# Chunked scan of the second model: first inverse built earlier, outer products spread over the levels

## The chip, the cores and the metric

The kernel runs on one core of a Trainium2 chip. The metric is the device time of one execution in microseconds (us). TensorE does the matrix products into PSUM banks, VectorE and ScalarE (ACT) work on PSUM and SBUF, SyncE issues DMAs. The engines meet through semaphores alone.

## The reference, cut to what matters

Two models of two layers each run one after the other, over 512 tokens of width 1024. The second one's layers contain a recurrence over time for eight heads of size 64:

```
state = state * w_t - (state . kk_t) (a_t * kk_t) + v_t k_t
y_t   = state . r_t
```

The kernel computes it in chunks of 64 tokens. Inside a chunk the tokens depend on each other through a strictly triangular 64 x 64 matrix A per head (products of kk and a*kk), and the chunk needs the inverse of (1 + A). With it, U = inverse x (kk . state + AK . v), the new state = (state + k v - b U) x decay, and y = r . state + PK . v - PB . U, where AK, PK and PB are masked products ("outer" ones) of k or b with kk or r. Nothing of this is left out in either kernel.

## The kernel before, in words

`scan` is called once in each of the second model's two layers, so twice in an execution. Two of the eight heads lie on the two halves of the 128 partitions ("h"), the other factor is four pairs ("pr"). Four groups g of two chunks (cc = 0, 1) are worked off; both chunks of a group are inverted together, then the state passes through them one after the other. TensorE's and VectorE's orders are written out by hand: `pe_part` and `dve_part` are the two queues, and each engine takes its instructions in that order, waiting at semaphores. ACT only copies y out (L2797).

The steps by line, all matmuls being 64 x 64 fp32:
- L2716, `products(g, bank)`: 16 matmuls into one bank: A (bank 0), its transpose (1), AK (2), PK (3), PB (4). An fp32 matmul leaves two records in the trace, so one call is 32 records, a half of it 16.
- L2808: A is masked into SBUF. L2812 and L2813 cut out the first level of A and its transpose for one chunk, L2815 makes the first inverse of it (identity minus that) into XX[cc], which holds the inverse and its transpose side by side, 256 columns each.
- L2820 to L2822: AK, PK and PB are masked into SBUF; `outer` says that TensorE has made them, `prod_used` that they have been read.
- Levels: the inverse doubles its block size five times (2 to 32). For each: L2735, W = A x inverse (8 matmuls a chunk), L2828, W is masked; L2743 and L2745, the two products that give the correction of the inverse and of its transpose (8 matmuls each, a chunk); L2831, it is subtracted, 512 columns wide. x_ok counts inverses ready, w_ok masked Ws.
- Serial part, for each chunk: L2756 and L2758 right-hand side, L2837 copy, L2768 U, L2839 copy, L2780 and L2782 state product, L2841 add, L2843 multiply with the decay (s_ok). L2703 to L2705, `y_pairs`, are the products for y, dealt out over the waits. The next group's products 0, 1 and 2 are put there too.

Between the groups the queues have, in this order: TensorE: y of chunk 1, a wait for ACT's copy of y, outer products 3 and 4 of the next group, first W. VectorE: state multiply, mask of A, both first inverses, the three outer masks, first W mask. In the diff's PSUM use, bank 5 is W of chunk 0 and right-hand side, 7 is W of chunk 1 and state product, 6 is X of chunk 0 and U, 1 is X of chunk 1 and A's transpose.

Of the kernel before, what the change touches and what calls it, by code (L numbers as in the profile page):

```python
# [10 lines left out]
ALU = mybir.AluOpType  # L11
# [4 lines left out]
P = 128  # L16
# [19 lines left out]
CH = 64  # L36
NCH = S // CH
NP = 4
# [47 lines left out]
class Core:  # L86
# [11 lines left out]
    def sem(self, name):  # L98

        if name not in self.sems:  # L100
            if name not in self.idle and self.made < self.MOST:
                self.idle[name] = self.ctx.enter_context(self.nc.semaphore(name))
                self.made += 1
            self.sems[name] = self.idle.pop(name if name in self.idle else next(iter(self.idle)))
        if name not in self.used and not name.startswith(self.LASTING):
            self.used.append(name)
        return self.sems[name]
# [2074 lines left out]
class Second(Kernel):  # L2182
# [490 lines left out]
    def scan(self):  # L2673
# [3 lines left out]
        nc, core, ps, A = self.nc, self.core, self.ps, self.arena  # L2677
# [16 lines left out]
        units = [(cc, pr, h) for cc in (0, 1) for pr in range(NP) for h in (0, 1)]  # L2694
        pairs = [(pr, h) for pr in range(NP) for h in (0, 1)]
        cols = lambda cc, pr: slice((cc * NP + pr) * CH, (cc * NP + pr) * CH + CH)

        def y_pairs(g, cc, pr):

# [6 lines left out]
            return last  # L2706

        def pe_part(pe):
            def products(g, bank):

                for cc, pr, h in units:
                    q, col = self.halves(h), (cc * NP + pr) * CH
                    tok = slice((2 * g + cc) * CH, (2 * g + cc) * CH + CH)
                    r, k, b, kk = (A[q, x + pr, tok] for x in (self.R, self.K, self.B, self.KK))
                    lhs, rhs_ = ((b, kk), (kk, b), (k, kk), (k, r), (b, r))[bank]
                    last = nc.tensor.matmul(ps[q, bank, col:col + CH], lhs, rhs_, start=True, stop=True)  # L2716
                return last
# [4 lines left out]
            products(0, 2)  # L2722
            pe.wait_ge(sem("tm_used"), 12)
            for g in range(4):
                if g:
                    pe.wait_ge(y_used, 2 * g)
                products(g, 3)
                products(g, 4).then_inc(outer, 1)

                for n, lv in enumerate(LEVELS):  # L2730
                    for cc in (0, 1):
                        pe.wait_ge(x_ok, 12 * g + 2 * n + cc + 1)
                        for pr, h in pairs:
                            q, col, o = self.halves(h), cols(cc, pr), slice(pr * CH, pr * CH + CH)
                            last = nc.tensor.matmul(ps[q, w_bank[cc], o], AT[q, col], XX[cc][q, o],  # L2735
                                                    start=True, stop=True)
                        last.then_inc(w_ps, 1)
                    for cc in (0, 1):
                        pe.wait_ge(w_ok, 10 * g + 2 * n + cc + 1)
                        for pr, h in pairs:  # L2740
                            q, col, o = self.halves(h), cols(cc, pr), slice(pr * CH, pr * CH + CH)
                            ot = slice(256 + pr * CH, 256 + pr * CH + CH)
                            nc.tensor.matmul(ps[q, x_bank[cc], o], XX[cc][q, ot], W[q, col],  # L2743
                                             start=True, stop=True)
                            last = nc.tensor.matmul(ps[q, x_bank[cc], ot], W[q, col], XX[cc][q, ot],  # L2745
                                                    start=True, stop=True)
                        last.then_inc(x_ps, 1)
# [52 lines left out]
        def dve_part(dve):  # L2800
            tt_, stt_ = nc.vector.tensor_tensor, nc.vector.scalar_tensor_tensor
            half = lambda v, cc: v.rearrange("p (c n) -> p c n", c=2)[:, cc, :]
            dve.wait_ge(sem("tm_turned"), 12)
            nc.vector.memset(state[0], 0.0).then_inc(s_ok, 1)
            for g in range(4):
                dve.wait_ge(prod, g + 1)
                dve.drain()
                tt_(as3(AT), as3(ps[:, 0, :]), wide(self.c("upper")), ALU.mult)  # L2808
                level1 = self.c("level1").unsqueeze(1).to_broadcast([P, NP, CH])
                level1t = self.c("levelT1").unsqueeze(1).to_broadcast([P, NP, CH])  # L2810
                for cc in (0, 1):
                    tt_(as3(half(XX[cc], 0)), as3(half(ps[:, 1, :], cc)), level1, ALU.mult)  # L2812
                    tt_(as3(half(XX[cc], 1)), as3(half(ps[:, 0, :], cc)), level1t, ALU.mult)  # L2813
                    dve.drain()
                    tt_(as3(XX[cc]), wide(self.c("ident2")), as3(XX[cc]), ALU.subtract)  # L2815
                    dve.drain().then_inc(x_ok, 1)
                dve.wait_ge(outer, g + 1)
                if g:
                    dve.wait_ge(y_ps, 2 * g)
                tt_(as3(AKT), as3(ps[:, 2, :]), wide(self.c("upper")), ALU.mult)  # L2820
                tt_(as3(PKT), as3(ps[:, 3, :]), wide(self.c("upper_eq")), ALU.mult)
                stt_(as3(PBT), as3(ps[:, 4, :]), -1.0, wide(self.c("upper_eq")), ALU.mult, ALU.mult)  # L2822
                dve.drain().then_inc(prod_used, 1)
                for n, lv in enumerate(LEVELS):
                    level = self.c(f"level{lv}").unsqueeze(1).to_broadcast([P, NP, CH])
                    for cc in (0, 1):
                        dve.wait_ge(w_ps, 10 * g + 2 * n + cc + 1)
                        tt_(as3(half(W, cc)), as3(ps[:, w_bank[cc], 0:256]), level, ALU.mult).then_inc(w_ok, 1)  # L2828
                    for cc in (0, 1):
                        dve.wait_ge(x_ps, 10 * g + 2 * n + cc + 1)  # L2830
                        tt_(XX[cc], XX[cc], ps[:, x_bank[cc], :], ALU.subtract)  # L2831
                        dve.drain().then_inc(x_ok, 1)
                for cc in (0, 1):
                    c = 2 * g + cc
                    old, new = state[cc], state[1 - cc]
                    dve.wait_ge(r_ps, c + 1)
                    nc.vector.tensor_copy(rhs, ps[:, 5, 0:256]).then_inc(r_ok, 1)  # L2837
                    dve.wait_ge(u_ps, c + 1)
                    nc.vector.tensor_copy(U[cc], ps[:, 6, 0:256]).then_inc(u_ok, 1)  # L2839
                    dve.wait_ge(s_ps, c + 1)  # L2840
                    tt_(new, old, ps[:, 7, 0:256], ALU.add)  # L2841
                    dve.drain()
                    tt_(as3(new), as3(new), egl[:, :, c:c + 1].to_broadcast([P, NP, CH]), ALU.mult)\  # L2843
                        .then_inc(s_ok, 1)

        return Parts(None, pe_part, act_part, dve_part)


# [603 lines left out]
```

## Time and profile before

| | |
|---|---|
| three runs, median | 3784.06 us (3781.48 to 3784.39) |
| profiled execution | 3784.52 us |
| its span in the trace | 3782.7 us |
| TensorE busy | 3664.8 us, 97% |
| VectorE busy | 2174.3 us, 57% |
| ACT busy | 1367.3 us, 36% |
| mean granted clock of TensorE | 0.982 |
| the two scans | about 2284 to 2427 us and 3139 to 3282 us |

The profile is one execution seen by the hardware profiler. A timeline row gives start, duration, engine, line, operation, operands, and in brackets how long the engine was idle before and what released it. Rows of several records (x16) give the stretch that they fill together; the last matmul's end is modelled. DMA hardly moves in the scans. The 1.8 us between the span and the execution's time lie around the program.

### The profile page before, as it was taken

The page shows a single profiled execution, that of the slowest core. Times are in us where ns is not written, and L with a number is a line of the kernel's source. Part 1 is how long each engine was busy: PE and PEld are TensorE (multiplying, and loading weights), DVE is VectorE, ACT ScalarE, POOL GpSimd, SP SyncE. Part 2 cuts the span into 40 slices and gives each one's busy share as a digit, 9 for nine tenths or more (in the row PEclk, how much of TensorE's full clock was granted, in tenths as well). Part 3 has the DMA queues.
Part 4 walks back from the last instruction along what each step waited for, and adds up shares of the span by engine and source line. Part 5 has one row for each costly group of instructions (what it writes and reads, how often), then busy time and mean ns, then how long its engine had stood idle before and what let it go on. Part 6 is the DMA issues. An engine that isn't in the chain of part 4 may idle for free. (4 is left out here: it accounts for less than half of the span.)

```text
span 3782.7 us, 57931 instructions
## 1 busy us (share of the span) xinstructions
PE 3664.8 (97%) x24033; PEld 3028.9 (80%) x24033; DVE 2174.3 (57%) x2934; ACT 1367.3 (36%) x1537; POOL 0.2 (0%) x4
## 2 busy tenths in 40 slices
PE   7999999999999999999999998999999998899998
PEld 6788888888877888888887768888887768888887
DVE  6898466774369964667634565553234575553233
ACT  5554433432264544343323341133223351123223
POOL 0000000000000000000000000000000000000000
PEclk9999999999999999999999999999999999999999
DMA  3322223553322222245522420123232320032321
GB/s 112 87 73 62 78 89 110 202 189 122 94 78 81 67 68 78 94 151 189 198 89 71 132 79 26 36 101 99 90 100 81 111 99 26 25 111 89 100 94 73
DMA packets 272985, 364.68 MB, mean 96 GB/s; under 512 B 22428, under 2 KB 218640, under 8 KB 271504
## 3 DMA queue, kind: packets, MB, share of 16 engines
q1 hardware_dynamic: 247824, 311.45, 25.7%
q10 hardware_dynamic: 24960, 50.33, 3.8%
q8 instruction: 153, 2.51, 0.3%
q14 instruction: 48, 0.39, 0.0%
HBM read 351.79 MB, written 9.96 MB: 96 GB/s over the span
## 5 line engine op out<-in xcount | busy, mean ns | idle before, releaser
L248 PE MATMUL banks<-act_hi,w_hi 128*128 128x512 f32 x4208 | 1675.2, 398 | 32.1 <-issue 9.9
L250 PE MATMUL banks<-act_hi,w_lo 128*128 128x512 f32 x4208 | 1647.9, 392 | 0.0
L249 PE MATMUL banks<-act_lo,w_hi 128*128 128x512 f32 x4208 | 1647.5, 392 | 0.0
L170 DVE TENSOR_TENSOR w_lo<-w_raw,w_hi 128x2048 fp32r<-128x2048 f32 (+1 forms) x280 | 629.4, 2248 | 666.8 <-ACT w_hi L164 662.6
L248 PEld LDWEIGHTS banks<-act_hi,w_hi 128*128 128x128 f32 x4208 | 795.5, 189 | 237.1 <-issue 59.0
L250 PEld LDWEIGHTS banks<-act_hi,w_lo 128*128 128x128 f32 x4208 | 794.7, 189 | 169.9
L249 PEld LDWEIGHTS banks<-act_lo,w_hi 128*128 128x128 f32 x4208 | 796.0, 189 | 165.1 <-issue 4.3
L164 ACT ACTIVATE w_hi<-w_raw 128x2048 fp32r<-128x2048 f32 (+1 forms) x280 | 526.5, 1881 | 932.8 <-PE banks L250 891.4
L2064 DVE SCALAR_TENSOR_TENSOR arena<-arena,small 128x512 f32<-128x512 f32 (+1 forms) x168 | 126.3, 752 | 15.6 <-issue 4.3
L248 PE MATMUL banks<-w_hi,act_hi 128*128 128x256 f32 x384 | 110.3, 287 | 3.2 <-DVE w_lo L170 3.2
L249 PE MATMUL banks<-w_lo,act_hi 128*128 128x256 f32 x384 | 108.6, 283 | 0.0
L250 PE MATMUL banks<-w_hi,act_lo 128*128 128x256 f32 x384 | 108.6, 283 | 0.0
L2797 ACT ACTIVATE arena<-banks 128x256 f32<-128x256 f32 x16 | 6.1, 383 | 279.2 <-PE banks L2705 279.2
L2743 PE MATMUL banks<-arena 64*64 64x64 f32 x1280 | 85.1, 229 | 14.9 <-DVE arena L2828 14.9
L2984 DVE TENSOR_TENSOR arena<-banks,arena 128x512 f32 (+1 forms) x44 | 30.4, 692 | 117.0 <-PE banks L250 116.3
L2743 PEld LDWEIGHTS banks<-arena 64*64 64x64 f32 x1280 | 78.2, 139 | 16.0 <-DVE arena L2828 16.0
L1869 ACT ACTIVATE arena<-banks 128x512 f32<-128x512 f32 (+3 forms) x64 | 28.1, 438 | 164.6 <-PE banks L1832 164.6
L2745 PE MATMUL banks<-arena 64*64 64x64 f32 x1280 | 83.3, 225 | 0.0
L2053 DVE SCALAR_TENSOR_TENSOR arena<-arena,param_cols 128x512 f32<-128x512 f32 x96 | 72.2, 752 | 19.0 <-issue 18.4
L2023 ACT ACTIVATE arena<-banks 128x512 f32<-128x512 f32 x48 | 28.7, 599 | 149.0 <-PE banks L250 148.7
L2050 DVE TENSOR_SCALAR arena<-arena,param_cols 128x512 f32<-128x512 f32 x48 | 26.2, 547 | 96.1 <-ACTq L2025 94.0
L695 DVE TENSOR_TENSOR act_lo<-arena,act_hi 128x1024 fp32r<-128x1024 f32 (+1 forms) x64 | 76.0, 1187 | 7.7 <-ACT act_hi L690 7.4
(363 smaller groups left out, 3592.7 us busy)
## 6 DMA issues: line engine op xcount, KB each, us to landing
w_raw<-in_w_in SPq DMA_DIRECT2D x98, 1024.0 KB, 5.4
w_raw<-in_ffn_up SPq DMA_DIRECT2D x48, 1024.0 KB, 5.4
arena<-in_ada_w ACTq DMA_DIRECT2D x24, 2048.0 KB, 8.0
w_raw<-in_w_gu SPq DMA_DIRECT2D x44, 1024.0 KB, 5.0
w_raw<-in_ffn_down SPq DMA_DIRECT2D x24, 1024.0 KB, 4.8
w_raw<-in_w_down SPq DMA_DIRECT2D x20, 1024.0 KB, 5.0
w_raw<-in_w_out SPq DMA_DIRECT2D x16, 1024.0 KB, 4.9
w_raw<-in_w_branch SPq DMA_DIRECT2D x12, 1024.0 KB, 5.0
```

Source lines behind the costliest of these rows:

```text
L164: self.core.nc.scalar.activation(view(self.hi[:, s]), view(self.raw[:, s]), ACT.Copy)\
L170: self.core.nc.vector.tensor_tensor(view(self.lo[:, s]), view(self.raw[:, s]), view(self.hi[:, s]).bitcast(FP32), ALU.subtract)\
L248: nc.tensor.matmul(out, wh, ah, start=first, stop=False)
L249: nc.tensor.matmul(out, wh, al, start=False, stop=False)
L250: return nc.tensor.matmul(out, wl, ah, start=False, stop=last)
L695: k.nc.vector.tensor_tensor(k.lo[:, self.at(i, s), :], self.source(i, s), k.hi[:, self.at(i, s), :].bitcast(FP32), ALU.subtract).then_inc( ...
L2023: nc.scalar.activation(pad[t][:, 3:3 + S], ps[:, t, :], ACT.Copy)\
L2053: ins = nc.vector.scalar_tensor_tensor(g[t], pad[t][:, 1 + k:1 + k + S], w[k], g[t], ALU.mult, ALU.add)
L2064: ins = nc.vector.scalar_tensor_tensor(dst, ada_w[:, k, :], c_act[:, k:k + 1], acc, ALU.mult, ALU.add)
L2743: nc.tensor.matmul(ps[q, x_bank[cc], o], XX[cc][q, ot], W[q, col], start=True, stop=True)
L2745: last = nc.tensor.matmul(ps[q, x_bank[cc], ot], W[q, col], XX[cc][q, ot], start=True, stop=True)
L2984: nc.vector.tensor_tensor(dst, ps[:, 2 + t, :], g[t], ALU.mult).then_inc(used, 1)
```

## The change

- The next group's mask of A and both first inverses go from the start of the group into the serial part of the group before, between its copies and adds (`a_mask`, `first_level`, `first_inverse`). Group 0 has them in front, as before.
- Outer products 3 and 4 are halved and each half is put between W of chunk 0 and W of chunk 1 in levels 0 to 3. With them goes the wait for ACT's copy of y. The first W of chunk 1 now waits for the state, because it shares bank 7.
- The three outer masks are put behind the W masks of levels 0, 2 and 4 (`outer_mask`).
- The last level leaves out L2743, the product for the inverse that isn't transposed, since only the transposed one is used afterwards; its subtraction is 256 columns wide.

The diff, cut to its core:

```diff
         def pe_part(pe):
...
             for g in range(4):
-                if g:
-                    pe.wait_ge(y_used, 2 * g)
-                products(g, 3)
-                products(g, 4).then_inc(outer, 1)
-
                 for n, lv in enumerate(LEVELS):
                     for cc in (0, 1):
+                        if cc and n < 4:
+                            if g and n % 2 == 0:
+                                pe.wait_ge(y_used, 2 * g - 1 + n // 2)
+                            last = products(g, 3 + n // 2, units[n % 2 * 8:n % 2 * 8 + 8])
+                            if n % 2:
+                                last.then_inc(outer, 1)
                         pe.wait_ge(x_ok, 12 * g + 2 * n + cc + 1)
+                        if g and cc and n == 0:
+                            pe.wait_ge(s_ok, 2 * g + 1)
...
-                            nc.tensor.matmul(ps[q, x_bank[cc], o], XX[cc][q, ot], W[q, col],
-                                             start=True, stop=True)
+                            if n < LAST:
+                                nc.tensor.matmul(ps[q, x_bank[cc], o], XX[cc][q, ot], W[q, col],
+                                                 start=True, stop=True)
...
         def dve_part(dve):
+            def a_mask(g):
+                dve.wait_ge(prod, g + 1)
+                tt_(as3(AT), as3(ps[:, 0, :]), wide(self.c("upper")), ALU.mult)
+
+            def first_level(cc):
+                tt_(as3(half(XX[cc], 0)), as3(half(ps[:, 1, :], cc)), level1, ALU.mult)
+                tt_(as3(half(XX[cc], 1)), as3(half(ps[:, 0, :], cc)), level1t, ALU.mult)
+
+            def first_inverse(cc):
+                dve.drain()
+                tt_(as3(XX[cc]), wide(self.c("ident2")), as3(XX[cc]), ALU.subtract)
+                dve.drain().then_inc(x_ok, 1)
+
+            def outer_mask(g, n):
+
+                if n == 0:
+                    tt_(as3(AKT), as3(ps[:, 2, :]), wide(self.c("upper")), ALU.mult)
+                elif n == 2:
+                    dve.wait_ge(outer, 2 * g + 1)
+                    if g:
+                        dve.wait_ge(y_ps, 2 * g)
+                    tt_(as3(PKT), as3(ps[:, 3, :]), wide(self.c("upper_eq")), ALU.mult)
+                elif n == 4:
+                    dve.wait_ge(outer, 2 * g + 2)
+                    stt_(as3(PBT), as3(ps[:, 4, :]), -1.0, wide(self.c("upper_eq")), ALU.mult, ALU.mult)\
+                        .then_inc(prod_used, 1)
...
             for g in range(4):
...
                         tt_(as3(half(W, cc)), as3(ps[:, w_bank[cc], 0:256]), level, ALU.mult).then_inc(w_ok, 1)
+                    outer_mask(g, n)
+                    new = slice(256 if n == LAST else 0, 512)
                     for cc in (0, 1):
                         dve.wait_ge(x_ps, 10 * g + 2 * n + cc + 1)
-                        tt_(XX[cc], XX[cc], ps[:, x_bank[cc], :], ALU.subtract)
+                        tt_(XX[cc][:, new], XX[cc][:, new], ps[:, x_bank[cc], new], ALU.subtract)
                         dve.drain().then_inc(x_ok, 1)
...
                     nc.vector.tensor_copy(rhs, ps[:, 5, 0:256]).then_inc(r_ok, 1)
+                    if cc and g < 3:
+                        first_inverse(0)
                     dve.wait_ge(u_ps, c + 1)
                     nc.vector.tensor_copy(U[cc], ps[:, 6, 0:256]).then_inc(u_ok, 1)
+                    if g < 3:
+                        if cc:
+                            first_level(1)
+                            first_inverse(1)
+                        else:
+                            a_mask(g + 1)
                     dve.wait_ge(s_ps, c + 1)
...
                         .then_inc(s_ok, 1)
+                    if cc == 0 and g < 3:
+                        first_level(0)
```

## Rows read from the trace of the kernel before

**Rows 1.** The page, part 1: busy time, share of the span, instructions
```profile
PE 3664.8 (97%) x24033; PEld 3028.9 (80%) x24033; DVE 2174.3 (57%) x2934; ACT 1367.3 (36%) x1537; POOL 0.2 (0%) x4
```

**Rows 2.** Timeline of VectorE, serial stage: start, us, line, [idle before <-releaser]
```profile
2314.38 0.42 DVE L2841 TENSOR_TENSOR arena<-arena,banks 128x256 f32<-128x256 f32 x1 [1.44 <-PE banks L2782]
...
2316.59 0.42 DVE L2837 COPY arena<-banks 128x256 f32<-128x256 f32 x1 [1.29 <-PE banks L2758]
...
2317.80 0.42 DVE L2839 COPY arena<-banks 128x256 f32<-128x256 f32 x1 [0.78 <-PE banks L2768]
...
2320.17 0.42 DVE L2841 TENSOR_TENSOR arena<-arena,banks 128x256 f32<-128x256 f32 x1 [1.95 <-PE banks L2782]
2320.68 0.43 DVE L2843 TENSOR_TENSOR arena<-arena,small 128x256 f32<-128x256 f32 x1
```

**Rows 3.** Timeline of VectorE, prologue of group 1
```profile
2321.19 0.69 DVE L2808 TENSOR_TENSOR arena<-banks,consts 128x512 f32<-128x512 f32 x1
2321.80 0.41 DVE L2812 TENSOR_TENSOR arena<-banks,consts 128x256 f32<-128x256 f32 x1
...
2327.14 0.76 DVE L2828 TENSOR_TENSOR arena<-banks,consts 128x256 f32<-128x256 f32 x2
```

**Rows 4.** Timeline of TensorE, the same stretch
```profile
2312.26 1.15 PE L2716 MATMUL banks<-arena 64*64 64x64 f32 x32
...
2321.26 0.28 PE L2705 MATMUL banks<-arena 64*64 64x64 f32 x2
...
2327.62 0.34 PE L2743 MATMUL banks<-arena 64*64 64x64 f32 x4 [1.91 <-DVE arena L2828]
```

**Rows 5.** Timeline of both engines, the second level of group 0
```profile
2295.14 0.68 PE L2735 MATMUL banks<-arena 64*64 64x64 f32 x16
...
2296.07 0.68 PE L2735 MATMUL banks<-arena 64*64 64x64 f32 x16 [0.25 <-DVEq L2832]
...
2296.11 0.42 DVE L2828 TENSOR_TENSOR arena<-banks,consts 128x256 f32<-128x256 f32 x1
...
2296.59 0.34 PE L2743 MATMUL banks<-arena 64*64 64x64 f32 x4
...
2296.80 0.42 DVE L2828 TENSOR_TENSOR arena<-banks,consts 128x256 f32<-128x256 f32 x1 [0.27 <-PE banks L2735]
...
2297.82 0.69 DVE L2831 TENSOR_TENSOR arena<-arena,banks 128x512 f32<-128x512 f32 x1 [0.59 <-PE banks L2745]
...
2298.76 0.69 DVE L2831 TENSOR_TENSOR arena<-arena,banks 128x512 f32<-128x512 f32 x1 [0.25 <-PE banks L2745]
...
2299.56 0.42 DVE L2828 TENSOR_TENSOR arena<-banks,consts 128x256 f32<-128x256 f32 x1
```

**Rows 6.** Timeline of both engines, group 0 of both scans
```profile
2287.95 2.60 PE L2716 MATMUL banks<-arena 64*64 64x64 f32 x82 [1.71 <-issue]
...
2289.03 0.69 DVE L2815 TENSOR_TENSOR arena<-consts,arena 128x512 f32<-128x512 f32 x1
...
2293.14 0.34 PE L2743 MATMUL banks<-arena 64*64 64x64 f32 x4 [1.60 <-DVE arena L2828]
...
3143.51 0.69 DVE L2815 TENSOR_TENSOR arena<-consts,arena 128x512 f32<-128x512 f32 x1
...
3146.82 0.34 PE L2743 MATMUL banks<-arena 64*64 64x64 f32 x4 [1.85 <-DVE arena L2828]
```

**Rows 7.** Timeline of VectorE in group 2; windows (busy of PE, PEld, DVE, ACT, POOL; PEclk)
```profile
2362.00 0.76 DVE L2828 TENSOR_TENSOR arena<-banks,consts 128x256 f32<-128x256 f32 x2
...
2363.86 0.69 DVE L2831 TENSOR_TENSOR arena<-arena,banks 128x512 f32<-128x512 f32 x1 [1.11 <-PE banks L2745]
...
2365.57 0.69 DVE L2831 TENSOR_TENSOR arena<-arena,banks 128x512 f32<-128x512 f32 x1 [1.02 <-PE banks L2745]
...
2369.97 0.42 DVE L2828 TENSOR_TENSOR arena<-banks,consts 128x256 f32<-128x256 f32 x1
...
2364.00:2366.00 2.00, 2.00 (x44) 2.00 (x41) 0.98 (x2) 0.00 (x0) 0.00 (x0) 0.50 0.00 0
```

More of the change, by code:

```diff
@@ L2696, in scan @@
         cols = lambda cc, pr: slice((cc * NP + pr) * CH, (cc * NP + pr) * CH + CH)
+        LAST = len(LEVELS) - 1
         def y_pairs(g, cc, pr):
@@ L2708, in pe_part, with products @@
         def pe_part(pe):
-            def products(g, bank):
-                for cc, pr, h in units:
+            def products(g, bank, part=units):
+                for cc, pr, h in part:
                     q, col = self.halves(h), (cc * NP + pr) * CH
@@ L2802, in dve_part @@
             half = lambda v, cc: v.rearrange("p (c n) -> p c n", c=2)[:, cc, :]
+            level1 = self.c("level1").unsqueeze(1).to_broadcast([P, NP, CH])
+            level1t = self.c("levelT1").unsqueeze(1).to_broadcast([P, NP, CH])
+            def a_mask(g):
[4 more added lines that the diff above has]
+                tt_(as3(half(XX[cc], 1)), as3(half(ps[:, 0, :], cc)), level1t, ALU.mult)
@@ L2803, in dve_part @@
             dve.wait_ge(sem("tm_turned"), 12)
             nc.vector.memset(state[0], 0.0).then_inc(s_ok, 1)
-            for g in range(4):
[L2806 to L2823, printed above, removed]
@@ L2824, in dve_part @@
+            dve.drain()
+            a_mask(0)
+            for cc in (0, 1):
+                first_level(cc)
+                first_inverse(cc)
+            for g in range(4):
                 for n, lv in enumerate(LEVELS):
```

## The prediction

> **What bounds the kernel now.** I read the page first. TensorE is busy for 97% of the span [rows 1], which says little here: the diff touches only the scan of the second model, which runs twice (about 2284 to 2427 us and 3139 to 3282 us). So I read the order of instructions of VectorE in one pass from group 0 to group 1, then that of TensorE in the same place, then one level of the inverse, then the two starts and the granted clock.
>
> The scan has four groups, and each has three stages. *Serial*: state to right-hand side to U to state, twice; it ends with the state multiply, at 2320.68 + 0.43 = 2321.11 [rows 2]. *Prologue*: VectorE masks A, builds the first inverse of both chunks and reads out three outer products one after the other; the first level mask comes at 2327.14, 6.03 us after the state [rows 3]. TensorE stands idle 1.91 us before its first X product at 2327.62 [rows 4]. The prologue is bound by VectorE. *Levels*: five equal ones. One cycle runs from W mask (2296.11) to the next (2299.56), 3.45 us, and passes through both X products and the second subtraction [rows 5]: TensorE first, then VectorE.
>
> **Rate of TensorE in the scan.** An fp32 matmul leaves two records. The second subtraction starts 0.94 after the first, which is X of chunk 1, 32 records: 29.3 ns a record. 16 records are 0.47 us, and a chunk's result reaches VectorE 0.29 after the last record's turn (2296.59 + 32 x 0.0293 + 0.29 = 2297.82, as in [rows 5]).
>
> **Part 1: the prologue goes, groups 1 to 3.** What moves into the serial part, with its cover on VectorE (0.08 stands for a drain: 2320.17 + 0.42 to 2320.68):
> - A's mask (0.69): its product is complete at 2312.26 + 1.15 = 2313.41 [rows 4], so it ends at about 2314.14. The add of chunk 0 comes at 2314.38 [rows 2]. Slack 0.24.
> - First level of chunk 0 (two of 0.41): from about 2315.22 to 2315.95, the copy at 2316.59 [rows 2]. Slack 0.6.
> - First inverse of chunk 0 (0.69 and two drains): 2317.09 to 2317.86 against the U copy at 2317.80 [rows 2]. It makes that copy 0.06 late. TensorE is in between with products of the next group, and VectorE afterwards idles 1.95 until the add [rows 2], so the chain does not feel it.
> - First level and inverse of chunk 1: 2318.19 to 2319.78, the add at 2320.17 [rows 2]. Slack 0.39. The state multiply stays at 2320.68.
>
> So the serial part keeps its length. TensorE issues its last y records at 2321.26 and 2321.29 [rows 4]. Behind them come W of chunk 0 (16 records), half of outer product 3 (16), W of chunk 1 (16). The waits in between are met: the inverse of chunk 1 at 2319.78, the state at 2321.11, ACT's read of bank 3 long before. 2321.34 + 48 x 0.0293 = 2322.75, and 0.05 to hand over gives the first X product at 2322.80 in place of 2327.62 [rows 4]: 4.82 us. The mask of AK (0.69) lies behind the W masks, see part 3. There are six such boundaries; between the same two kinds of rows the prologues last 6.03 [rows 3], 6.40, 6.04, 6.13, 6.04 and 6.03, sum 36.67. What takes their place is 6.03 - 4.82 = 1.21 each. Gain 36.67 - 7.26 = **29.4**.
>
> **Part 2: group 0 of both scans.** The first inverse stays in front, the three outer masks go. The inverse of chunk 1 ends at 2289.03 + 0.69 + 0.08 = 2289.80; W of chunk 1 (0.47) and the 0.05 put X at 2290.33 instead of 2293.14. In the second scan: 3143.51 + 0.77 + 0.53 = 3144.81 instead of 3146.82 [rows 6]. Gain 2.8 + 2.0 = **4.8**.
>
> **Part 3: outer masks and products in the levels.** A half product is 16 records, 0.47, and goes between W of chunk 0 and W of chunk 1. These now start at 2295.14 and 2296.07 [rows 5]: 0.93 apart, of which the first takes 0.47, so the hole is 0.46. Overrun 0.01, for 24 halves (levels 1 to 3, eight groups) 0.2; from the other side, 0.05 each if a semaphore read comes on top, 1.2. I take 0.2. No nearer row shows a gain.
> The masks of AK and PK (0.69, levels 0 and 2) start 0.34 after the second W mask (2296.80), at 2297.14. An independent operation may start before the one in front of it ends: the mask of 0.69 at 2321.19 is followed at 2321.80, 0.61 later [rows 3]. So the subtraction could start at 2297.75 and is needed at 2297.82 [rows 5]. They fit, with under 0.1 to spare.
> The Trainium skill (VectorE: DVE Perf Modes, The DRAIN you can't avoid) speaks against this: it lets the next operation start only when the pipe has emptied. By that every mask would push the subtraction by about 0.09 in 16 levels and by 0.16 in 8, some 2.7 us less gain. The row with 0.61 decides against it; its section on two Vector instructions with no wait between them has the exception.
>
> **Part 4: the last level.** The X product without transpose is left out: X is 16 records a chunk, the subtractions are 256 wide (0.42, as the W mask of that width) [rows 5]. PB's mask is put there. Counted from the first W mask: second W mask at 0.69, PB's mask at 1.03, first subtraction at 1.64 (the product was ready at 1.24), second at 2.14 (ready at 1.92), done 2.56, TensorE goes on at 2.64. Before: second subtraction at 2.65, done 3.34, TensorE at 3.41. Gain 0.77 x 8 = **6.2**. Here VectorE is last, not TensorE; without the mask it would be about 1.0.
>
> **Part 5: the clock.** In five of six boundaries, all but the first, TensorE fell to half clock just after the prologue: granted 0.50 from 2364 to 2366, that is 1.2 of 2.4 GHz. There the subtractions are 1.71 apart instead of 0.94, and two levels take from 2362.00 to 2369.97, 7.97 instead of 6.91 [rows 7]. Cost 1.06; the five together, in the same way, 1.06 + 1.30 + 1.06 + 1.39 + 1.07 = **5.9**. Before each, TensorE had waited repeatedly, last for 1.9 us [rows 4]. Within unbroken level stretches, with a hole of 0.25 a level, none falls. The change takes exactly those holes away, so I expect the spells to go.
> The Trainium skill (TensorE: Matmul & The Clock Gate, What's actually happening) says that idleness brings the low clock and sustained work releases it. The same page (A second HAM failure mode) says that small idles between groups of matmuls are enough to swing it. By the first the 5.9 come back, by the second they need not; that is the first rival.
>
> **Sum.** 29.4 + 4.8 + 6.2 - 0.2 = 40.2, with the clock 46.1. The profiled execution took 3784.5, so 3738.4; the median of the runs is 0.5 lower, so **3738.0**. After the scan nothing else changes: its last group keeps its order, and weights were loaded before it.
>
> **Rivals.**
> - *The spells stay.* Holes remain: about 1.0 us of TensorE idle at each group's end, longer than now (0.81). For it: five of six boundaries had one. Against it: they came only behind prologues. 40.2 gain, 3743.9.
> - *The moved work is not hidden.* Slacks of 0.24 and -0.06 are thin. If all of it, 0.69 + 4 x 0.41 + 2 x 0.69 and no overlap, 3.7 us a boundary, came on the serial chain: 6 x 3.7 = 22, 3760. Against it: idle times of 1.44, 1.29, 0.78 and 1.95 in front of the four operations [rows 2].
> - *Slower: TensorE at half clock through the levels.* The prologue was VectorE's; now the levels with their short holes follow each other with nothing between. At half clock 32 records cost 1.71 - 0.94 = 0.77 more [rows 7, 5], 24 ns each. On the path of a group lie 4 x 80 + 48 = 368, so 8.8 us, for eight groups 71. If all levels were low: 71 - 40.2 = 31 slower, 3815. It decides from 57% of the level time on. Against it: the levels of all groups ran at full clock once a spell was over.
> - That the change doesn't do what it says I leave out: the order of both queues is written out.
>
> **How the numbers follow.** Forecast 0.75, spells stay 0.17, moved work on the chain 0.05, half clock 0.03. Around the forecast itself: above it the products' other bound (1.0), one more stall on the issue of instructions like the 1.71 us in the first scan [rows 6], and the runs' own scatter (2 to 3 us between three runs), together up to 4; below it the last level without its mask's hold (0.26 x 8 = 2) and the same scatter, together up to 4. With the first rival and 2 above it the range is 3734 to 3746. A measurement can tell about 0.2% (7.6 us) from no change. Faster by more than that: the first three, 0.97; the last case is split, 0.01 within and 0.02 slower.
>
> **What the profile after would show.** First X product of a group 1.7 us after the state multiply ends, not 6.5; A's mask and first inverse inside the serial stage with the state multiply still 5.8 after that of chunk 0; level cycles 3.45 with 16 product records in the hole; a last level of 2.64; granted clock 1.00 through the scan. Wrong would be: idle time of TensorE in front of the s or u products that VectorE's new work ends, level cycles over 3.5, or 0.50 in the clock.

## The result

| | median of the runs | ratio to the kernel before, 95% interval |
|---|---|---|
| before | 3784.22 us (3781.48 to 3786.08) | |
| changed | 3737.39 us (3735.61 to 3738.30) | 0.9877 [0.9866, 0.9888] |

The changed kernel is 46.8 us faster; 46.1 were forecast. Its profiled execution took 3735.61. The page of the changed kernel, total and part 1, to be set beside [rows 1]: 256 records fewer on TensorE, which is the last level's product (128 matmuls of two records), and 25 us less busy time.

```profile
span 3733.8 us, 57413 instructions
...
PE 3639.4 (97%) x23777; PEld 3009.4 (81%) x23777; DVE 2168.7 (58%) x2934; ACT 1367.5 (37%) x1537; POOL 0.2 (0%) x4
```

The two scans, from the state's memset to the first operation behind them, took 142.3 and 142.4 us before, together 284.6, and take 120.4 and 118.8 now, together 239.2: 45.4 of the 48.9 by which the two profiled executions differ. The other 3.5 lie in unchanged code (the first scan starts at 2282.0, at 2285.0 before), within what single executions scatter.

Timeline of VectorE of the changed kernel, from the serial part of group 0 to group 1 (start, us, line, idle before and releaser). In its lines L2813 is A's mask, L2816 and L2817 the first level, L2821 the first inverse, L2861 the right-hand side's copy, L2865 U's copy, L2873 and L2875 the state's add and multiply, L2850 the W mask, L2827 AK's mask, L2855 the subtraction:

```profile
2308.27 0.69 DVE L2813 TENSOR_TENSOR arena<-banks,consts 128x512 f32<-128x512 f32 x1 [0.51 <-PE banks L2717]
2309.20 0.42 DVE L2873 TENSOR_TENSOR arena<-arena,banks 128x256 f32<-128x256 f32 x1 [0.24 <-PE banks L2787]
...
2311.42 0.42 DVE L2861 COPY arena<-banks 128x256 f32<-128x256 f32 x1 [0.62 <-PE banks L2763]
2311.94 0.69 DVE L2821 TENSOR_TENSOR arena<-consts,arena 128x512 f32<-128x512 f32 x1
2312.75 0.42 DVE L2865 COPY arena<-banks 128x256 f32<-128x256 f32 x1
...
2313.91 0.69 DVE L2821 TENSOR_TENSOR arena<-consts,arena 128x512 f32<-128x512 f32 x1
2315.00 0.42 DVE L2873 TENSOR_TENSOR arena<-arena,banks 128x256 f32<-128x256 f32 x1 [0.39 <-PE banks L2787]
2315.50 0.42 DVE L2875 TENSOR_TENSOR arena<-arena,small 128x256 f32<-128x256 f32 x1
2316.87 0.42 DVE L2850 TENSOR_TENSOR arena<-banks,consts 128x256 f32<-128x256 f32 x1 [0.94 <-PE banks L2739]
...
2318.14 0.68 DVE L2827 TENSOR_TENSOR arena<-banks,consts 128x512 f32<-128x512 f32 x1
2318.74 0.68 DVE L2855 TENSOR_TENSOR arena<-arena,banks 128x512 f32<-128x512 f32 x1
...
2320.47 0.42 DVE L2850 TENSOR_TENSOR arena<-banks,consts 128x256 f32<-128x256 f32 x1
```

This is what stands in place of [rows 2, 3]. A's mask, the first levels and both inverses lie between the copies and adds, and the idle time in front of those has shrunk: 0.24 before the add of chunk 0 (1.44 before), 0.62 before the copy (1.29), 0.12 before U's copy, too short to be shown in its row (0.78), 0.39 before the add of chunk 1 (1.95). The state's multiply of chunk 1 comes 5.79 after that of chunk 0 (2309.71, not shown), as before. The first W mask follows the end of the state's multiply by 0.95, not 6.03. AK's mask at 2318.14 is followed by the subtraction at 2318.74, 0.60 later.

The last level of group 0, VectorE and then TensorE's next product. L2835 is PB's mask, and the two subtractions of 256 columns are one row:

```profile
2302.04 0.42 DVE L2850 TENSOR_TENSOR arena<-banks,consts 128x256 f32<-128x256 f32 x1
2302.73 0.42 DVE L2850 TENSOR_TENSOR arena<-banks,consts 128x256 f32<-128x256 f32 x1 [0.27 <-PE banks L2739]
2303.07 0.68 DVE L2835 SCALAR_TENSOR_TENSOR arena<-banks,consts 128x512 f32<-128x512 f32 x1
2303.67 0.95 DVE L2855 TENSOR_TENSOR arena<-arena,banks 128x256 f32<-128x256 f32 x2
```

```profile
2304.70 0.34 PE L2761 MATMUL banks<-arena 64*64 64x64 f32 x4 [0.81 <-DVEq L2856]
```

2302.04 to 2304.70 is 2.66. Before, it was 3.41, from this row of VectorE to this one of TensorE:

```profile
2306.47 0.42 DVE L2828 TENSOR_TENSOR arena<-banks,consts 128x256 f32<-128x256 f32 x1
...
2309.88 0.34 PE L2756 MATMUL banks<-arena 64*64 64x64 f32 x4 [0.81 <-DVEq L2832]
```

In the changed kernel no gap stands in front of the subtractions: VectorE is last here, behind the mask.

Windows of the changed kernel (busy of PE, PEld, DVE, ACT, POOL, then PEclk): the start of the first scan, the rest of it, the second scan.

```profile
core 0: us, PE busy (x) PEld busy (x) DVE busy (x) ACT busy (x) POOL busy (x), PEclk, DMA share, GB/s
2286.00:2291.00 5.00, 4.59 (x102) 4.45 (x100) 2.87 (x6) 0.00 (x0) 0.00 (x0) 0.66 0.11 37
2300.00:2400.00 100.00, 93.61 (x2900) 90.29 (x2898) 63.15 (x127) 2.70 (x7) 0.00 (x0) 1.00 0.03 8
3115.00:3230.00 115.00, 106.82 (x3318) 103.20 (x3313) 75.36 (x150) 2.31 (x6) 0.00 (x0) 1.00 0.05 14
```

A stretch at half clock, as in [rows 7], is called a spell from here on. The spells are gone behind all six boundaries. One is left, in group 0 of the first scan, where this trace of the kernel before had none; its first level took 4.95 instead of 3.45.

### The profile page after: what moved, and what is told of

It reads as the page before. It is cut to its first block and busy times, and to the rows that moved or that the text cites. A ratio compares the mean times of both kernels' runs of the same rounds, so it can differ in the third digit from the quotient of the medians.

```text
span 3733.8 us, 57413 instructions
## 1 busy us (share of the span) xinstructions
PE 3639.4 (97%) x23777; PEld 3009.4 (81%) x23777; DVE 2168.7 (58%) x2934; ACT 1367.5 (37%) x1537; POOL 0.2 (0%) x4
## 5 line engine op out<-in xcount | busy, mean ns | idle before, releaser
L1903 DVE TENSOR_TENSOR arena<-banks,arena 128x512 f32<-128x512 f32 (+3 forms) x64 | 31.3, 488 | 83.9 <-PE banks L1806 81.5
L248 PEld LDWEIGHTS banks<-w_hi,act_hi 128*128 128x128 f32 x384 | 73.6, 192 | 7.4 <-DVE w_lo L170 4.1
L690 ACT ACTIVATE act_hi<-arena 128x1024 fp32r (+2 forms) x64 | 64.9, 1020 | 38.6 <-PE banks L250 38.6
```

Source lines behind the costliest of these rows:

```text
L248: nc.tensor.matmul(out, wh, ah, start=first, stop=False)
L690: self.k.nc.scalar.activation(self.k.hi[:, self.at(i, s), :], self.source(i, s), ACT.Copy).then_inc(self.hi_ok, 1)
L1903: nc.vector.tensor_tensor(prob[c % 2][:, 0:n], ps[:, 4 + 3 * (h % 2), 0:n], A[:, self.SC + qt, 0:n], ALU.add).then_inc(biased, 1)
```

## The experiments

Behind each time stands its ratio to the kernel before, which ran beside it, with the 95% interval. The first four experiments share one median of the kernel before (3783.6), the next three another (3785.0), the last two a third (3784.0). Each kernel was also read by stage in one trace. "Boundary" is the time from the end of the state's multiply to the next first W mask, "last level" that from the last level's first W mask to the right-hand side's copy, "serial" from that copy to the end of the second state multiply. In the kernel before they are 6.03 to 6.40, 4.65 and 9.98, in the changed one 0.85 to 0.95, 3.90 and 9.98.

### Filling TensorE's hole in the kernel before

```diff
                         last.then_inc(w_ps, 1)
+                    if n == 0:
+                        for pr, h in pairs * 3 + pairs[:4]:
+                            q, col, o = self.halves(h), cols(0, pr), slice(pr * CH, pr * CH + CH)
+                            nc.tensor.matmul(ps[q, x_bank[0], o], AT[q, col], XX[0][q, o],
+                                             start=True, stop=True)
```

> The kernel before, with 28 idle products (56 records, 1.64 us) put on TensorE between the first level's W and X products, in the hole of 1.9 us at the end of each prologue, into a bank that nobody reads. Nothing is left out of the result. Theory (TensorE's waiting in the prologue brings the low clock): granted clock 1.00 behind all prologues, two levels 6.91 us where the kernel before had 7.97, and 5.9 us less: 3778.3. Rival (the spells come with VectorE's part or with the start of the levels, whatever TensorE does in the hole): four to six spells stay, 3784.2. If the filling itself were late, X would start over 0.48 us after the first W mask; neither expects that.

Measured: 3778.5 us (before 3783.6), 0.9986 [0.9977, 0.9996]. Group 2 of the first scan, TensorE, then VectorE. The 56 filling records (L2741) stand where the hole of 1.9 was, and the first X product waits 0.27:

```profile
2359.53 0.68 PE L2735 MATMUL banks<-arena 64*64 64x64 f32 x16 [0.84 <-DVEq L2821]
2360.04 1.80 PE L2741 MATMUL banks<-arena 64*64 64x64 f32 x56
2362.11 0.34 PE L2748 MATMUL banks<-arena 64*64 64x64 f32 x4 [0.27 <-DVE arena L2833]
```

```profile
2361.63 0.76 DVE L2833 TENSOR_TENSOR arena<-banks,consts 128x256 f32<-128x256 f32 x2
...
2368.53 0.42 DVE L2833 TENSOR_TENSOR arena<-banks,consts 128x256 f32<-128x256 f32 x1
```

From W mask 2361.63 to 2368.53 two levels take 6.90, where [rows 7] has 7.97. Windows of this kernel's scans, behind the first group's start, with the columns as above:

```profile
2300.00:2420.00 120.00, 107.22 (x3258) 102.09 (x3252) 67.49 (x130) 2.31 (x6) 0.00 (x0) 1.00 0.02 4
3140.00:3275.00 135.00, 121.03 (x3667) 115.07 (x3665) 77.37 (x148) 2.69 (x7) 0.00 (x0) 1.00 0.05 16
```

No spell behind any of six boundaries, and none in the two groups 0. The first level of the first scan took 4.31 instead of 3.45, but not by the clock: TensorE stopped for 1.08 within the filling, with nothing in the profile to wait for ("issue"), at a granted clock of 1.00. That is a stall as the 1.71 in [rows 6]. TensorE's row, and the window over group 0:

```profile
2291.54 1.44 PE L2741 MATMUL banks<-arena 64*64 64x64 f32 x42 [1.08 <-issue]
```

```profile
2280.00:2300.00 20.00, 17.77 (x572) 17.20 (x569) 13.67 (x23) 4.22 (x6) 0.00 (x0) 1.00 0.32 108
```

The boundaries themselves stayed at 6.04 to 6.40. The two scans are 5.9 shorter than in the trace of the kernel before, as much as its five spells cost; the 0.9 of this stall stands against 0.8 for the one in [rows 6]. So in these traces the gain is clock, TensorE's waiting in the prologue is a cause of the spells, and filling it without any use of the work is worth some 5 us. The mean granted clock of all executions goes the same way, 0.9828 over ten against 0.9800 over nineteen, though in a single execution it says little: 0.981 in this trace without a spell, 0.982 in the trace before with five.

### The last level alone

```diff
-                            nc.tensor.matmul(ps[q, x_bank[cc], o], XX[cc][q, ot], W[q, col],
-                                             start=True, stop=True)
+                            if n < 4:
+                                nc.tensor.matmul(ps[q, x_bank[cc], o], XX[cc][q, ot], W[q, col],
+                                                 start=True, stop=True)
...
+                    new = slice(256 if n == 4 else 0, 512)
...
-                        tt_(XX[cc], XX[cc], ps[:, x_bank[cc], :], ALU.subtract)
+                        tt_(XX[cc][:, new], XX[cc][:, new], ps[:, x_bank[cc], new], ALU.subtract)
```

> The kernel before, with only the last level changed: no product for the untransposed inverse, subtraction 256 columns wide. The outer masks stay in the prologue. Theory (in the changed kernel PB's mask holds the last level on VectorE): here the last level takes 2.42 us from its first W mask to TensorE's next product, not 3.41, 0.99 x 8 = 7.9 us less, 3776.3. Rival (the mask costs nothing, something else sets the 2.66 of the changed kernel): 2.66 here too, 6.0 less, 3778.2. Clock spells as in the kernel before in both.

Measured: 3772.3 us, 0.9975 [0.9966, 0.9985]. The last level of group 0, VectorE (L2829 W mask, L2833 subtraction) and TensorE's next product:

```profile
2306.74 0.42 DVE L2829 TENSOR_TENSOR arena<-banks,consts 128x256 f32<-128x256 f32 x1
...
2307.95 0.42 DVE L2833 TENSOR_TENSOR arena<-arena,banks 128x256 f32<-128x256 f32 x1
2308.64 0.42 DVE L2833 TENSOR_TENSOR arena<-arena,banks 128x256 f32<-128x256 f32 x1 [0.27 <-PE banks L2746]
```

```profile
2309.14 0.34 PE L2757 MATMUL banks<-arena 64*64 64x64 f32 x4 [0.55 <-DVEq L2834]
```

2306.74 to 2309.14 is 2.40, where the changed kernel has 2.66. The last level is 3.64 in all eight groups, 1.01 below 4.65: 8.1 us. The time fell by 11, some 3 more than the stage gives; its trace has four spells where that of before has five (0.9 us), the rest is within the interval. The theory holds: PB's mask costs 0.26 a group in the changed kernel.

### The changed kernel with the last level whole

```diff
-                            if n < LAST:
+                            if n <= LAST:
...
-                    new = slice(256 if n == LAST else 0, 512)
+                    new = slice(0, 512)
```

> The changed kernel with the last level's product and full-width subtraction put back. Theory (term of the last level 0.77 x 8): last level 3.41 to 3.45 us, 6.2 more than the changed kernel, 3743.6, and no clock spells between the groups: they went with the prologue. Rival (the shorter last level is what cured the clock): spells of 1.0 to 1.4 us come back behind boundaries, up to 3750.

Measured: 3744.3 us, 0.9901 [0.9884, 0.9917], 6.9 above the changed kernel. The last level is 4.65 again in all groups, 0.75 more than 3.90: 6.0. All first levels stood between 3.45 and 3.61, and the granted clock was 1.00 from group 0 on in both scans. So the shorter last level isn't what took the spells away in this trace.

### PB's mask one level earlier

```diff
-                elif n == 4:
+                elif n == 3:
                     dve.wait_ge(outer, 2 * g + 2)
```

> The changed kernel with PB's mask in level 3 instead of the last. Theory (it holds the last level's subtraction): last level 2.42 instead of 2.66, level 3 stays 3.45, 8 x 0.24 = 1.9 less, 3735.5. Rival (no slack in level 3, the mask moves the same cost there): level 3 at 3.5 to 3.7, no gain, 3737.4.

Measured: 3732.5 us, 0.9873 [0.9856, 0.9889]. VectorE in level 3 and the start of the last level:

```profile
2299.08 0.42 DVE L2850 TENSOR_TENSOR arena<-banks,consts 128x256 f32<-128x256 f32 x1
...
2300.11 0.68 DVE L2835 SCALAR_TENSOR_TENSOR arena<-banks,consts 128x512 f32<-128x512 f32 x1
2300.79 0.69 DVE L2855 TENSOR_TENSOR arena<-arena,banks 128x512 f32<-128x512 f32 x1
...
2302.53 0.42 DVE L2850 TENSOR_TENSOR arena<-banks,consts 128x256 f32<-128x256 f32 x1
```

The mask at 2300.11 stands in front of the subtraction at 2300.79, and the level still takes 3.45 (2299.08 to 2302.53). The last level is 3.64 as in the kernel without the mask there, 0.26 less than 3.90, 2.1 us in all. The trace shows that gain; the times (4.9 below the changed kernel, with four runs from 3731.0 to 3738.0) don't resolve it. A mask of 0.68 is free in any level with the full product and costs 0.26 in the short one.

### Only the inverse moved; only the outer products spread

In the first, VectorE's part is that of the changed kernel in the serial stage, and in front of each group stand the old wait for `outer` and the three masks. The second is the changed kernel with this edit and with the last level whole, as in the third experiment; in front of the loop over the groups the first inverse is taken out as well:

```diff
             for g in range(4):
+                a_mask(g)
+                for cc in (0, 1):
+                    first_level(cc)
+                    first_inverse(cc)
...
-                    if cc and g < 3:
-                        first_inverse(0)
...
-                    if g < 3:
-                        if cc:
-                            first_level(1)
-                            first_inverse(1)
-                        else:
-                            a_mask(g + 1)
...
-                    if cc == 0 and g < 3:
-                        first_level(0)
```

> The kernel before with only the first inverse moved into the serial part; outer products and the three masks stay in front of the levels, the last level is whole. Theory (each part alone leaves another thing late): the first W mask comes 5.0 us after the state multiply instead of 6.0, because ACT's copy of y, 64 product records and then three masks follow each other; 6 x 1.0 = 6 us less, 3778. TensorE idles some 1.8 us before X as before, so half-clock spells stay in several of six boundaries. Rival (the moved inverse is the gain, the spreading only tidies): most of 29.4 us, about 3755.

Measured: 3771.8 us (before 3785.0), 0.9966 [0.9954, 0.9979]. Group 2 of the first scan, VectorE and TensorE:

```profile
2358.97 0.69 DVE L2832 TENSOR_TENSOR arena<-banks,consts 128x512 f32<-128x512 f32 x1 [2.96 <-PE banks L2716]
...
2360.97 0.75 DVE L2840 TENSOR_TENSOR arena<-banks,consts 128x256 f32<-128x256 f32 x2
```

```profile
2356.84 2.08 PE L2716 MATMUL banks<-arena 64*64 64x64 f32 x64 [0.47 <-ACT arena L2799]
...
2361.45 0.34 PE L2745 MATMUL banks<-arena 64*64 64x64 f32 x4 [1.60 <-DVE arena L2840]
```

VectorE (L2832 the first of the three masks) now waits 2.96 us for the outer products (L2716) and then makes the three masks; the boundary is 5.05 (4.97 once). The six fell by 6.5 together. Group 0 of the first scan fell by 0.9, of which 0.8 is only that the stall of [rows 6] didn't come. What I got wrong is the clock: no spell at all, though TensorE still waited 1.60 before X. That is the remaining 5.9, and the time came 6 lower than I had written. No run shows why this wait, and not the 1.91 of the kernel before, was without a spell.

> The changed kernel with the first inverse back at the start of each group and the last level whole; outer products and masks stay spread. Theory: first W mask about 3.9 us after the state multiply, then level 1 with half a product; per boundary 2.1 us less than the kernel before, with group 0 (4.8) 17 us less, 3767; TensorE now idles some 2 us at the start of the boundary, so spells can stay. With the run before this one it adds up to 23 of the 34 us that both moves together give: the rest comes only when both are gone. Rival (terms are additive): 28 us less, 3756.

Measured: 3761.3 us, 0.9937 [0.9920, 0.9953]. TensorE waits for the inverse at the boundary of group 2:

```profile
2354.11 0.73 PE L2739 MATMUL banks<-arena 64*64 64x64 f32 x16 [2.03 <-DVEq L2822]
```

```profile
2355.00:2359.00 4.00, 3.95 (x89) 3.76 (x87) 2.66 (x5) 0.00 (x0) 0.00 (x0) 0.62 0.00 0
```

The boundary is 3.78 to 3.79, with waits of 1.67 and 0.49, but for this one, which is 4.14 with a single wait of 2.03. The six are together 13.6 below those before; the two groups 0 are 5.0 below, 0.8 of it the stall that didn't come. Spells: behind three of six boundaries and in group 0 of the first scan, 5.2 us. The whole scans are 19.3 shorter by the trace, 17 were expected. The time is 23.7 lower, with an interval from 18 to 30. That holds the rival's 28 too, so the time alone doesn't decide against terms that simply add up; the boundaries in the trace do.

The two halves give 6.5 and 13.6 at the boundaries. With both, the six boundaries lose 31.1, and the first level behind each gets 0.15 longer (3.60 or 3.61), 30.2 net. The half product alone isn't the reason: in group 0 and with the spreading alone the first level has it too and takes 3.45 or 3.46. There TensorE still waits 0.41 to 0.49 for the inverse of chunk 1 behind the half product; at the boundaries of the changed kernel it waits for nothing there, and the half product delays the W behind it. So 10.1 come only when both are done: with the inverse early the outer products and masks are late, with these spread the inverse is.

### The products out of the serial part

On top of PB's mask in level 3:

```diff
+                        elif cc and g < 3:
+                            products(g + 1, 2, units[:8])
                         pe.wait_ge(x_ok, 12 * g + 2 * n + cc + 1)
...
+                if g < 3:
+                    products(g + 1, 2, units[8:])
+                    products(g + 1, 0, units[:6])
                 pe.wait_ge(x_ok, 12 * g + 12)
...
                     elif g < 3:
-                        products(g + 1, 0)
+                        products(g + 1, 0, units[6:])
+                        products(g + 1, 1, units[:3])
...
-                        if g < 3:
-                            products(g + 1, 2)
                     elif g < 3:
-                        products(g + 1, 1).then_inc(prod, 1)
+                        products(g + 1, 1, units[3:]).then_inc(prod, 1)
```

> PB's mask in level 3, and the next group's products 0, 1 and 2 dealt out by the holes: product 2 and part of 0 into the last level, the rest into the two holes of chunk 0 in the serial part, none in chunk 1. Theory: the serial part of groups 0 to 2 is 1.0 us longer than that of group 3 only because TensorE is in these products when the right-hand side and U are ready; it falls from 9.98 to about 9.1, last level up by at most 0.05; 5.3 less than the variant with the mask in level 3, some 3727 to 3728. Rival (VectorE's moved inverse now holds U's copy and the add, since no product covers it): serial part stays over 9.6, at most 2 less, 3731.

Measured: 3731.5 us, 0.9856 [0.9840, 0.9873]. Serial part 9.40 (9.98 before, 9.1 expected), last level 3.69. VectorE in chunk 1 of group 0 (L2865 right-hand side's copy, L2825 inverse, L2869 U's copy, L2877 add):

```profile
2315.75 0.42 DVE L2865 COPY arena<-banks 128x256 f32<-128x256 f32 x1 [0.62 <-PE banks L2768]
2316.27 0.69 DVE L2825 TENSOR_TENSOR arena<-consts,arena 128x512 f32<-128x512 f32 x1
2317.08 0.42 DVE L2869 COPY arena<-banks 128x256 f32<-128x256 f32 x1
...
2319.05 0.42 DVE L2877 TENSOR_TENSOR arena<-arena,banks 128x256 f32<-128x256 f32 x1
```

U's copy comes 1.33 behind the right-hand side's (1.21 in group 3, which has no moved work), held by the inverse at 2316.27, which is issued in front of it; the add follows it by 1.97 (1.71 in group 3) without idle time. The products had covered this work of VectorE, and now it shows. From one first W mask to the next a group takes 27.85, 28.53 with PB's mask moved alone: 0.68 a group, 4.1 in all, not 5.3. The times of these two kernels overlap. In group 0 of the first scan this trace had a spell too, and in front of it a stop of TensorE of 1.82 with nothing in the profile to wait for.

### The inverses put behind what they held

```diff
-                    if cc and g < 3:
-                        first_inverse(0)
...
                             first_level(1)
-                            first_inverse(1)
+                            first_inverse(0)
...
                     if cc == 0 and g < 3:
                         first_level(0)
+                    elif g < 3:
+                        first_inverse(1)
```

> The kernel of the run before (products out of the serial part), with the first inverse of chunk 0 behind U's copy of chunk 1 and that of chunk 1 behind the state multiply. Theory (what kept that kernel's serial part at 9.39 instead of 9.0 is VectorE: U's copy 0.12 late behind the inverse, the state add 0.26 late behind the second one): U's copy again 1.21 and the add 1.71 behind it, serial part 9.0 to 9.05; the first W mask moves back to 0.95 behind the state multiply, because TensorE's y products set it; together 0.12 to 0.25 a boundary, 1 to 1.5 less in all, 3730, which the times can't resolve but the trace can. Rival (TensorE's y records or the semaphores hold them): serial part stays near 9.4.

Measured: 3730.2 us (before 3784.0), 0.9857 [0.9841, 0.9874]. The same stretch (U's copy is L2867, the add L2875, the W mask L2854, the inverse behind the state's multiply L2825):

```profile
2311.58 0.42 DVE L2865 COPY arena<-banks 128x256 f32<-128x256 f32 x1 [0.62 <-PE banks L2768]
2312.79 0.42 DVE L2867 COPY arena<-banks 128x256 f32<-128x256 f32 x1 [0.78 <-PE banks L2779]
...
2314.77 0.42 DVE L2875 TENSOR_TENSOR arena<-arena,banks 128x256 f32<-128x256 f32 x1
...
2315.78 0.69 DVE L2825 TENSOR_TENSOR arena<-consts,arena 128x512 f32<-128x512 f32 x1
2316.59 0.42 DVE L2854 TENSOR_TENSOR arena<-banks,consts 128x256 f32<-128x256 f32 x1
```

U's copy is back at 1.21. The add still comes 1.98 behind it: the first level and the inverse with their two drains start 0.34 behind the copy and take 1.64, together 1.98, more than the room of 1.71 that I had counted for them, and the serial part is 9.28, not 9.05. The first W mask comes 0.90 behind the state's multiply instead of 0.80. It isn't TensorE's y products that set it, as I had expected, but the inverse at 2315.78, which VectorE now makes in front of it. Still TensorE gains: the first X product of a group starts 5.49 behind the copy of the right-hand side, 5.59 in the run before, and the level behind the first W mask takes 3.50 instead of 3.61. A group (from one first W mask to the next) takes 27.72, 0.13 less than with the order before, which is about the 0.12 that U's copy had been late. This is the shortest of all variants by the trace.

### The changed kernel once more

> The changed kernel as it is, on the same chip as the run before it, for the comparison of both and to see whether the half-clock spell at the start of its first scan comes again. Theory (spells are a matter of the single execution where TensorE has waited): it may or may not come, stages elsewhere as in the first trace; 3737, and the reordered kernel 7 us below it. Rival (the spell belongs to the changed order of group 0): it comes again, 1.5 us, and in every trace.

Measured, the changed kernel unaltered: 3738.0 us, 0.9876 [0.9859, 0.9892]. The window over group 0 of the first scan up to its fourth level:

```profile
2283.00:2300.00 17.00, 15.45 (x488) 15.02 (x486) 13.14 (x24) 0.70 (x2) 0.00 (x0) 1.00 0.32 110
```

No spell this time (the first level 3.56, not 4.95), so the rival falls: the spell doesn't come with every execution of this order. Nor does it need it, as the kernel with only the last level changed had one in the same group. The reordered kernel is 7.8 us below it by the medians of the same chip, and 7.0 by the scans (237.8 to 230.8).

## Why the prediction was right, point by point

- **Rate and pattern.** 29.3 ns a record held: without a spell or a stall the levels before the last are 3.45 to 3.46 in every kernel. Exceptions are the first one behind a boundary of the changed order (3.60 or 3.61; 3.50 with the inverses reordered) and the first one of the first scan in two traces (3.56).
- **Part 1, boundaries.** Forecast 4.82 for the first. Boundary and first level together went from 9.49 to 4.55, 4.94. Six gave 30.2, 29.4 forecast. TensorE's W came 0.11 behind the state's multiply, where I had counted 0.23. I had put W behind the last y record, and the trace has its first records beside the last ones of y: W starts at 2316.03, the last y record at 2316.14. (The last y record of the kernel before starts at 2321.32; I had read 2321.29.) The serial part stayed 9.98 as said, with A's mask 0.24 ahead of the add, as computed, and U's copy late without effect. It was 0.12 late, not 0.06. The two runs with the products taken out showed that this cover was real: there a group is 0.13 shorter once that copy is no longer late.
- **Part 2, group 0.** Forecast 2.8 and 2.0. From the state's memset to the first W mask of the second level, the second scan went from 10.29 to 8.22, 2.07. The first scan went from 11.09 to 8.32 in the repeated execution, 2.8; in the first trace a spell took half of it. The 2.8 came out in part by luck: 0.8 of it is the stall of 1.71 in [rows 6], which belongs to that one execution and not to the prologue. The two other traces with the prologue of the kernel before reach the first W mask of the first scan 6.84 behind the memset, as all three do in the second scan, where that trace took 7.64; and a stall of 1.82 stood in one trace of the changed order too. What the change itself takes away is 2.1 in both scans. In the sum the 0.8 too much is hidden by the 0.8 that the boundaries gave above their forecast.
- **Part 3, levels.** No overrun could be seen: levels 1 to 3, which have half a product each, take 3.45 or 3.46. The masks of AK and PK are free. The row with 0.61 was right: the subtraction starts 0.60 behind the start of AK's mask of 0.68. The general rule of the Trainium skill (VectorE: DVE Perf Modes, The DRAIN you can't avoid), by which the next operation starts only when the pipe has emptied, doesn't hold for these pairs. By that rule I would have taken 2.7 less.
- **Part 4, last level.** Forecast 0.77 a group, measured 0.75; without the mask's hold 1.01, as said. The place that I named as last, VectorE behind PB's mask, was tested by taking the mask away in two kernels: both give 2.40 to 2.41 instead of 2.66.
- **Part 5, clock.** The spells behind the boundaries went, 5.9 back. Right in sign, place and size for this pair of traces; but it isn't a fixed sum. The kernel with only the last level changed had three of six, the one with only the outer products spread three. And a spell can stand in group 0 of the first scan, with the order before (last level alone) as with the changed one. It was there in four of eleven traces, in the changed kernel's first and not in its second, and cost 1.5 there.
- **The rivals.** Spells that stay: behind none of 36 boundaries in six traces of the changed order (the changed kernel twice, last level whole, PB's mask earlier, the two with products taken out). The wait behind the last level that I gave this rival as 1.0 is 0.81, as before. Moved work on the chain: no, though it is nearer than the idle times said, as the last two variants show. Half clock through the levels: no, 1.00 in both scans but for the spell in group 0.

What is not settled is how much waiting brings the clock down. Behind the state's multiply TensorE waits for 0.47, 0.47 to 0.84, and 1.91 in the kernel before (five of six boundaries with a spell) and, the same, with only the last level changed (three of six); for 1.67 and 0.49 with the spreading alone (two of five, and the one boundary with 2.03 had a spell too); for 0.47 and 1.60 with the inverse alone (none of six); for 0.47, 0.47 to 0.84, and 0.27 when filled (none of six); for nothing in the changed order (none of 36). On the whole more waiting went with more spells, but each kernel but the changed one has a single trace, and the same order of work has a spell at one boundary and not at the next. The filling shows that the wait is a cause; what decides at a given boundary no run shows.

## What to carry to other kernels

Where two engines hand each other a chain with a front part on one of them, count what is late once that part is gone: here either half of the move left the other in its place, and a third of the boundaries' gain came with both only. Work of 0.4 to 0.7 us put into an engine's measured idle time costs nothing as long as the other engine is the late one there; in the changed kernel the short last level was the one place where it wasn't, and a level with room for the mask gave 2 us more. A stall that stands in one trace is not a term of the change: measure the same stage in the second pass or in another trace before counting it. In a stretch of small matmuls, look at the granted clock behind each wait of TensorE before counting stage lengths: it was an eighth of this gain.

## What the runs showed of the hardware

Products that nobody reads, put into TensorE's wait, made the kernel faster: 3778.5 against 3783.6 [0.9977, 0.9996], by the clock staying at 2.4 GHz behind the boundaries, which themselves kept their length. The Trainium skill (TensorE: Matmul & The Clock Gate, A second HAM failure mode) tells of a bf16 kernel in which short idles between groups of matmuls were frequent enough to make the clock swing. This case's fp32 traces agree for the prologue, with waits of 0.47, 0.47 and 1.91, and not for the levels: a wait of 0.25 every 3.45 us, and 0.8 at each group's end, brought it down in no trace.

TensorE can stop in a row of matmuls with nothing in the profile to wait for: 1.71 us in the trace before, 1.08 in the filled kernel and 1.82 with the products out of the serial part, each in group 0 of the first scan. What stops it no run shows. A level lengthened by this looks like a spell (4.31 against 3.45 in the filled kernel, at a granted clock of 1.00), and the clock column tells them apart.
